# Rotated queries and keys added by TensorE, gates by Silu in one ScalarE pass

## The reference, cut to what matters

```
def _rope(x):
    ...
    x1, x2 = x32[..., : d // 2], x32[..., d // 2:]
    return jnp.concatenate([x1 * cos - x2 * sin, x1 * sin + x2 * cos], axis=-1).astype(x.dtype)

rq = _rope(proj[..., o_rq:o_rk].reshape(b, s, RET_HEADS, RET_HEAD_DIM))
rk = _rope(proj[..., o_rk:o_rv].reshape(b, s, RET_HEADS, RET_HEAD_DIM))
ret = _retention(rq, rk, rv)
ret = (_rms(ret) * ret_out_gain[l]).reshape(b, s, RET_WIDTH) * jax.nn.silu(r_gate.astype(jnp.float32))
...
return (o * jax.nn.silu(r)) @ w_out      # GLA, o is normalised and scaled by norm_g
```

## Time and profile before

| | |
|---|---|
| median of 3 runs | 991.39 us (990.47 to 992.85) |
| profiled execution, its own time | 991.15 us |
| its span, first to last instruction | 989.2 us |
| mean granted TensorE clock | 0.993 |
| busy: PE, DVE, ACT, POOL | 97%, 68%, 47%, 6% |

### The profile page before, as it was taken

How to read it: one execution, slowest core, us unless ns; L and a number is a source line. 1 busy time by engine, 2 the same in 40 slices (tenths; PEclk the granted TensorE clock), 3 DMA queues, 4 the chain that set the end, 5 groups by cost and what they waited for, 6 DMA issues and landing times.

```text
span 989.2 us, 13707 instructions
## 1 busy us (share of the span) xinstructions
PE 958.2 (97%) x4982; PEld 797.0 (81%) x4982; DVE 675.2 (68%) x875; ACT 463.4 (47%) x710; POOL 55.0 (6%) x61
## 2 busy tenths in 40 slices
PE   9999999999999999899899999998999999999996
PEld 7778877888888887777688888887776888888885
DVE  5868898895566576677976556667643876655657
ACT  5477535464445345544355444444652434544441
POOL 3040111200000001000200000000000010000000
PEclk9999999999999999999999999999999999999998
DMA  9979787596555676421375665564342537566541
GB/s 303 336 227 276 220 255 235 198 313 210 194 170 193 206 258 165 128 86 46 121 246 192 196 204 174 190 211 153 127 148 86 168 132 233 193 197 205 170 148 43
DMA packets 110053, 186.91 MB, mean 189 GB/s; under 512 B 8729, under 2 KB 67169, under 8 KB 109985
## 3 DMA queue, kind: packets, MB, share of 16 engines
q1 hardware_dynamic: 104800, 177.33, 55.1%
q0 software_dynamic: 2656, 8.54, 3.2%
q10 hardware_dynamic: 2544, 0.35, 0.2%
HBM read 185.15 MB, written 1.05 MB: 188 GB/s over the span
## 4 chain that ended last, share of the span: by engine, by line
PE 78%; DVE 11%; ACT 3%; issue 3%; DMA 2%; POOL 2%; SPq 0%; POOLq 0%; DVEq 0%; ACTq 0%
PE AT L1956 16%; PE PJ L1816 14%; PE PJ L1817 14%; PE PJ L1818 14%; PE AT L1960 8%; DVE wlo L1137 3%; POOL rstd L483 2%; ACT whi L600 1%; PE AT L1802 1%; DVE bn L1225 1%; DMA raw<-in_w_out_dram 1%; DMA raw<-in_w_ada_dram 1%; PE AT L1816 1%; PE AT L2065 1%; DVE x L1223 1%
## 5 line engine op out<-in xcount | busy, mean ns | idle before, releaser
L1137 DVE TENSOR_TENSOR wlo<-raw,whi 128x1024 fp32r<-128x1024 f32 x144 | 173.4, 1221 | 50.9 <-ACT whi L600 50.1
L1956 PE MATMUL AT<-hT,whi 128*128 128x512 f32 x720 | 179.5, 391 | 0.0
L1263 DVE TENSOR_TENSOR wlo<-raw,whi 128x1024 fp32r<-128x1024 f32 x144 | 169.6, 1219 | 0.0
L600 ACT ACTIVATE whi<-raw 128x1024 fp32r<-128x1024 f32 x144 | 146.6, 1054 | 40.1 <-DMA raw<-in_w_in_dram 28.8
L1816 PE MATMUL PJ<-whi,uhi 128*128 128x512 f32 x392 | 154.0, 393 | 0.4
L1817 PE MATMUL PJ<-wlo,uhi 128*128 128x512 f32 x392 | 153.0, 390 | 0.0
L1818 PE MATMUL PJ<-whi,ulo 128*128 128x512 f32 x392 | 152.6, 389 | 0.0
L1956 PEld LDWEIGHTS AT<-hT,whi 128*128 128x128 f32 x720 | 131.9, 188 | 25.3
L1816 PE MATMUL PJ<-whi,hT 128*128 128x512 f32 (+1 forms) x360 | 146.7, 407 | 4.7 <-DVE hT L1320 1.6
L1273 DVE TENSOR_TENSOR pr<-AT,pr 128x512 f32<-128x512 f32 x45 | 31.1, 691 | 169.0 <-ACT pr L655 169.0
L647 ACT ACTIVATE whi<-raw 128x1024 fp32r<-128x1024 f32 x144 | 140.7, 1049 | 0.3 <-DMA raw<-in_mlp_w_dram 0.3
(11 more groups left out here) (332 smaller groups left out, 995.9 us busy)
## 6 DMA issues: line engine op xcount, KB each, us to landing
raw<-in_mlp_w_dram SPq DMA_DIRECT2D x128, 512.0 KB, 4.8
raw<-in_w_in_dram SPq DMA_DIRECT2D x32, 512.0 KB, 6.4
raw<-in_w_ada_dram SPq DMA_DIRECT2D x32, 512.0 KB, 5.6
raw<-in_w_mlp_in_dram SPq DMA_DIRECT2D x32, 512.0 KB, 4.9
raw<-in_w_mlp_out_dram SPq DMA_DIRECT2D x32, 512.0 KB, 4.7
raw<-in_c_w_in_dram SPq DMA_DIRECT2D x24, 512.0 KB, 4.5
raw<-in_w_ada_dram SPq DMA_DIRECT2D x32, 256.0 KB, 6.6
raw<-in_a_w_in_dram SPq DMA_DIRECT2D x12, 512.0 KB, 5.2
```

The source lines that it names most:

```text
L600: nc.scalar.activation(whi[:, s % SPL, :], raw_slot(r), ACT.Copy).then_inc(hi_done, 1)
L1137: tt(wlo[:, n % SPL, :], raw_slot(r), whi[:, n % SPL, :].bitcast(F32), ALU.subtract).then_inc(raw_done, 1)
L1263: tt(wlo[:, s % SPL, :], raw_slot(r), whi[:, s % SPL, :].bitcast(F32), ALU.subtract)\
L1956: mm(out(f), whi[:, s % SPL, c(kk, f)], hT[:, k, :, :].rearrange("p a s -> p (a s)"), start=k == 0, stop=False, skip_group_check=True)
```

## The change

- `rotate` writes the cos part straight to `proj` and the sin part to `sc[:, t]`, and no longer adds them. For the keys it first waits for `rt_tr` (the turned queries of that tile), since `sc` is read by PE now; for the same reason ScalarE's `fox_squares(1)` waits for `rt_tr`.
- `turn` makes, per head, two fp32 matmuls with the identity that add up in PSUM, in place of one transpose.
- ScalarE computes Silu in place of Sigmoid for the retention and GLA gates and frees the PSUM banks itself. On DVE `ret_gates` goes, `r_gain` reads the finished gate from `proj`, and `gated` goes.

```diff
+            def silu(z, e):
+                return nc.scalar.activation(e, z, ACT.Silu)
             def gate_table():
-                gate(cst[:, C_ID:C_ID + 1], junk[:, :])
+                silu(cst[:, C_ID:C_ID + 1], junk[:, :])
...
                 act.wait_ge(sc_free, 4 + t)
+                if t:
+                    act.wait_ge(rt_tr, 1)
...
-                    gate(bank(7, t), proj[:, t, RG:RG + 512]).then_inc(gt_sig, 1)
+                    silu(bank(7, t), proj[:, t, RG:RG + 512]).then_inc(bank_free[1], 1)
...
-                    gate(bank(B_CIN + 4 + j, t), r_at(j, t)).then_inc(gt_sig, 1)
+                    silu(bank(B_CIN + 4 + j, t), r_at(j, t)).then_inc(bank_free[j], 1)
...
-                    a = sc[:, 0, :].rearrange("p (h d) -> p h d", h=4)
-                    c = sc[:, 1, :].rearrange("p (h d) -> p h d", h=4)
+                    a = proj[:, t, dst:dst + 512].rearrange("p (h d) -> p h d", h=4)
+                    c = sc[:, t, :].rearrange("p (h d) -> p h d", h=4)
+                    if k:
+                        dve.wait_ge(rt_tr, t + 1)
...
-                    link(tt(proj[:, t, dst:dst + 512], sc[:, 0, :], sc[:, 1, :], ALU.add))
...
-            def ret_gates():
-                for t in range(NT):
-                    o = proj[:, t, FK:FK + 512]
-                    dve.wait_ge(gt_sig, t + 1)
-                    tt(o, o, bank(7, t), ALU.mult).then_inc(bank_free[1], 1)
...
-                    dve.wait_ge(gt_sig, 2 + 2 * j + t + 1)
-                    tt(out_at(j, t).rearrange("p (h d) -> p h d", h=2),
-                             logit(j, t).rearrange("p (h d) -> p h d", h=2),
+                    dve.wait_ge(bank_free[j], B_CIN + 4 + t + 1)
+                    ins = tt(out_at(j, t).rearrange("p (h d) -> p h d", h=2),
+                             r_at(j, t).rearrange("p (h d) -> p h d", h=2),
...
-            def gated(j, t):
-                dve.wait_ge(gt_sig, 2 + 2 * j + t + 1)
-                tt(out_at(j, t), out_at(j, t), r_at(j, t), ALU.mult).then_inc(src_ready, 1)
...
-                    ins = nc.tensor.transpose(AT[:, f % 2, h * P:(h + 1) * P], proj[:, t, c0 + h * P:c0 + (h + 1) * P],
-                                              ident)
+                    o = AT[:, f % 2, h * P:(h + 1) * P]
+                    mm(o, proj[:, t, c0 + h * P:c0 + (h + 1) * P], ident, start=True, stop=False)
+                    ins = mm(o, sc[:, t, h * P:(h + 1) * P], ident, start=False, stop=True)
```

More of the change, by code:

```diff
@@ L260, in block_program @@
         dseq, aseq = sem("dseq"), sem("aseq")
-        gt_sig = sem("gt_sig")
         ffT_mm, ffT_done, ff_mm, ff_abs, ff_ln, ff_done, cum_mm, cum_done = [sem(n) for n in (
@@ L1474, in _ @@
                 28: [lambda: decayed(2), lambda: decayed(3)],
-                30: [ret_norm], 31: [ret_gates, ret_final],
+                30: [ret_norm], 31: [ret_final],
             })
@@ L1732, in _ @@
             r_at = lambda j, t: proj[:, t, 2048 + 512 * j:2048 + 512 * (j + 1)]
-            logit = lambda j, t: bank(B_CIN + 4 + j, t)
             out_at = lambda j, t: proj[:, t, half(j)]
@@ L1739, in r_gain @@
                 for t in range(NT):
-                    dve.wait_ge(gt_sig, 2 + 2 * j + t + 1)
-                    tt(out_at(j, t).rearrange("p (h d) -> p h d", h=2),
-                             logit(j, t).rearrange("p (h d) -> p h d", h=2),
-                             acc[:, NG:NG + 256].unsqueeze(1).broadcast_to([P, 2, 256]), ALU.mult).then_inc(bank_free[j], 1)
-                dve.wait_ge(bank_free[j], B_CIN + 4 + NT)
+                    dve.wait_ge(bank_free[j], B_CIN + 4 + t + 1)
+                    ins = tt(out_at(j, t).rearrange("p (h d) -> p h d", h=2),
+                             r_at(j, t).rearrange("p (h d) -> p h d", h=2),
+                             acc[:, NG:NG + 256].unsqueeze(1).broadcast_to([P, 2, 256]), ALU.mult)
+                link(ins)
             def gla_norm(j, t):
@@ L1753, in gla_norm, with gla_norms @@
                     ins = stt(o, AT[:, 2 * t + j, c], rstd[:, k:k + 1], o, ALU.mult, ALU.mult)
-                return ins
-            def gated(j, t):
-                dve.wait_ge(gt_sig, 2 + 2 * j + t + 1)
-                tt(out_at(j, t), out_at(j, t), r_at(j, t), ALU.mult).then_inc(src_ready, 1)
-            def gated_first():
-                for t in range(NT):
[L1763 to L1769, removed]
+                ins.then_inc(src_ready, 1)
+            def gla_norms(j):
+                for t in range(NT):
+                    gla_norm(j, t)
             tiles(T_CIN, T_COUT, {
@@ L1773, in _ @@
                 16: [lambda: state(0)], 17: [lambda: state(1)], 18: [lambda: state(2)],
-                19: [lambda: r_gain(0), lambda: gla_var(0)], 20: [lambda: gla_var(1), gated_first],
+                19: [lambda: r_gain(0), lambda: gla_var(0)], 20: [lambda: gla_var(1), lambda: gla_norms(0)],
                 22: [lambda: quarter_lo(7, 0), lambda: quarter_lo(7, 1)],
-                23: [lambda: r_gain(1), norm_second, lambda: gated(1, 0), lambda: gated(1, 1)],
+                23: [lambda: r_gain(1), lambda: gla_norms(1)],
             })
```

## The result

The changed kernel takes 995.07 us (median of 22 runs, 992.00 to 997.86); the kernel before, timed beside it, 992.57 us (22 runs, 989.95 to 994.93). The ratio is 1.0023, 95% interval [1.0013, 1.0033]. Over all three, the mean of its 46 runs is 994.84 and that of 116 runs of the kernel before is 992.85: +2.0 us, ratio 1.0020 [1.0015, 1.0026] (interval by resampling single runs, which leaves out the scatter between series). Taken by series, the means are 995.14, 994.52 and 994.61 with the change and 992.55, 992.34, 992.96, 994.02 and 993.38 without: each of the first lies above each of the second, and the difference of the two averages is +1.7. The change makes the kernel slower by 1.5 to 2 us; the forecast was +0.4 and a time of 991.8, and 995.07 is outside its range.

The account below looks back on a forecast made before the run. TensorE, busy 97% of the span, bounds the kernel. +5.3 - 2.5 - 1.7 = +1.2 us at 140 us, of which +0.4 reaches the end: 991.39 + 0.4 = 991.8 us, range 990.1 to 994.1.

Parts of the forecast that it names:

- the delay at the end of the first block: Rescaled x entering the first MLP: of PE's +1.2 us, DVE's own delay of +0.1 to +1.0 remains, taken at +0.4.
- the clock's credit: TensorE at 136 to 140 us: with no idle in front, the clock stays at 2.4 GHz, -1.7 us.
- PE's added work: Four turns of queries and keys: 32 product pairs at 0.217 us replace 16 transposes at 0.10, +5.3 us.
- The wait: PE's wait for DVE's rotation at the keys' turns goes entirely, -2.5 us, because PE is late, not only DVE early.
- rival 1: The clock falls all the same, at 136 to 140 us or nearby: 993.2 to 994.1 us, chance 0.13.
- PE's two waits: Ahead of the first MLP, for the rescaled x: 0.67 and 0.75 us start to start, absorbing part of PE's delay.
- rival 2: Before the first MLP, the last w_out tile lands later and PE waits instead: +1.0 to +2.5 us, chance 0.11.
- rival 3: By the first MLP all is hidden or a little gained, -0.2 at most by PE alone: 990 to 991.3, chance 0.13.
- rival 5: The change doesn't do what it says in the turns, adds and multiplies; given no chance.
- Gates: Silu removes 1.2 us of DVE multiplies at 163.61, offsetting DVE's +1.2 delay; the later GLA gates give nothing.
- The distance from M to the end: From the first MLP on the delay stays; wrong if it differs by over 0.5 us between 200 us and the end.

Follow-up runs that it names:

- e10: Changed kernel with only the keys turned by products, queries added and transposed as before, no filler products, GpSimd's two layer-norm broadcasts later: 992.86 us, ratio 1.0.
- e1: The kernel before once more, no edit: 994.35 us, ratio 1.0023 to the runs of the same kernel beside it.
- e6: The kernel before with GpSimd's two layer-norm row broadcasts issued later, behind its reciprocal roots: 991.85 us, ratio 0.999.
- e7: The kernel before with only the Silu gates of the change, and GpSimd's two layer-norm row broadcasts issued later: 992.28 us, ratio 0.9989.
- e12: The kernel before once more, no edit, a later repeat: 992.59 us, ratio 1.0005 to the kernel before.
- e4: The kernel before with only the Silu gates of the change, turns and rotation as before: 993.16 us, ratio 1.0013.
- e5: The changed kernel with GpSimd's two layer-norm row broadcasts issued later, behind its reciprocal roots: 992.79 us, ratio 1.0002.
- e3: The kernel before with only the turns by products and the rotation's sum of the change, gates as before: 993.83 us, ratio 1.0024.
- e2: The changed kernel once more, no edit: 994.82 us, ratio 1.0023 to the kernel before.
- e11: The changed kernel once more, no edit, a later repeat: 994.49 us, ratio 1.0014 to the kernel before.

## Why the prediction was wrong, point by point

In short: the term that failed is the delay at the end of the first block, taken at +0.4 us and measured at +1.35 in the two profiles that answer each other. Beside it the clock's credit of 1.7 us comes in some executions only, and 1.2 us of the miss in the total is the level of the three runs that the forecast started from.

**PE's added work, right.** 16 products take 3.55 and 3.57 us, 0.222 each, where 0.217 was used. Four turns cost 7.12 - 1.6 = +5.5 against +5.3. Of what the Trainium skill ("TensorE: Matmul & The Clock Gate", Terms) says, the transpose mode four times faster for fp32, the runs show 0.222 / 0.10 = 2.2 here, and rival 4 has fallen.

**The wait, right in size, wrong in its reason.** It left PE's list, and PE asked for nothing that was not ready. The prediction said that it goes "because PE is late, not only because DVE is early". Its own numbers say otherwise: the first turn ready at 132.80 and the second at 134.4, while PE without any delay is through the filler at 133.04 and through the first turn, eight products at 0.217, at 134.8. e10, read above, agrees: there the wait of 1.94 came back in place of a filler of 2.15. So by these numbers the credit of 2.5 us is DVE's, and it would stand with the queries' turns left alone.

**The clock, half right.** In the changed kernel it is 1.00 over 136 to 144, so the 1.7 us came back against the profile that was read; rival 1 did not happen. PE at K6 is 24.06 - 22.72 = +1.34, forecast +1.2. But the fall was taken as a property of the kernel before. With the original turns and rotation it came in before, e1, e6 and e7 and stayed away in e12 and e4. Against e12 PE is 24.05 - 21.09 = +2.96 late. On the mean of the three executions of the kernel before (22.13) it is +1.9. A credit that comes in some of the executions was booked in full. Whether a turn by products "would even work for the clock" no run decides; in e10 the clock fell during such a turn, behind the idle of 1.94.

**What the end of the block absorbs, wrong: this is the step that failed.** The prediction let the two releases before the removed multiplies cost "up to 1 us", took +0.4, on the reason that the transfer "has most likely used part of the idle DMA before 166", and let PE's two waits absorb the rest. The mechanism was seen (tiles released later, so that more bytes stand in front of the last one) and mis-sized. The DVE request did come as forecast (50.00 behind Q before, 50.13 after, so +0.1), and ScalarE's squares at +1.3 for the forecast +1.2. But the idle DMA lies in front of the restart (share 0.00 over 162.31 to 163.31, 0.65 in the microsecond behind it), not between the restart and the tile. The whole restart moved with PE, from 46.0 to 47.5, the landing by 57.43 to 58.78 = +1.35 and M by +1.38. That term is +1.35 in place of +0.4. Windows from the request of the tile to its landing, before and after, show the bytes:

```profile
167.31:174.74 7.43, 7.43 (x35) 5.53 (x34) 6.91 (x7) 2.04 (x3) 0.21 (x1) 1.00 0.96 274
```
```profile
170.73:179.38 8.65, 8.65 (x40) 6.58 (x39) 6.91 (x7) 2.98 (x4) 0.21 (x1) 1.00 0.98 314
```

That is 7.43 x 274 = 2.0 MB before and 8.65 x 314 = 2.7 MB after: 0.7 MB more had to pass, where up to 0.3 was counted. PE's two waits absorbed nothing, 0.53 and 0.59 as against 0.51 and 0.58, because what they wait for moved as much as PE did. This is rival 2 (+1.0 to +2.5, chance 0.11), as it was described. The agreement of +1.34 at K6, +1.35 at L and +1.38 at M is partly the luck of the pair: on the means of three executions each it is +1.9 at K6, +1.5 at L (57.34 to 58.82) and +1.5 at M, and against e1 alone L moves by just the +0.4 that was forecast. So of the mean +1.5, about 0.7 is the clock's credit booked in full, if that is handed on whole, and the other 0.8 stands where +0.4 was taken (an estimate).

**The other rivals.** Nothing was hidden or gained (rival 3): Q to M is longer than in every execution of the kernel before. Its "-0.2 at most" took both waits of PE, 1.42 us, as slack; e5 and e6 show that PE alone gives +0.4, since with the transfers away one wait of 0.4 stays. The change does what it says (rival 5): the turns and the missing rows stand in the trace.

**Gates, right within what can be told.** From Q to M e3 agrees with the changed kernel within 0.2 us and e7 with e6 within 0.02, though K6 is 0.25 earlier in e7: DVE's saved 1.2 us only let a tile be asked for earlier that lands no earlier. The GLA half changes no distance (763.15 in e4, 763.18 before).

**The distance from M to the end, wrong as a test.** It differed by 1.3 between the two profiles, more than the 0.5 allowed. That is the low clock at 416, which e12 has without the change.

**The level.** The three runs that gave 991.39 were low: 22 runs of the same kernel have 992.57. Of the 3.3 us between 991.8 and 995.07, 1.2 are this, and 2.1 the change's (2.5 in that series for 0.4). With the right term (+1.4) the forecast would have been 992.8; with the clock's credit at its mean, +1.5 to +2, still slower by less than the bound or just at it. The difference between the marks (+1.5) and the times (+1.7 to +2.0) stays open: it may be scatter between series, or the clock falling less often or more often in stretches that three profiles do not sample. In the timed runs the mean granted clock is no lower with the change (0.9920 in the 24 runs of e2 and e11, 0.9912 in 105 runs of the kernel before), so the added time is not a slower clock.

## What to carry to other kernels

Where an engine's lateness meets a stretch of saturated transfers, ask what restarts the transfers and how many bytes stand between the restart and the tile that is waited for, not only when that tile is asked for: a restart that hangs on the late engine handed on most of its delay here, and waits further down absorbed none of it. Before a wait is said to vanish because an engine is late, work out where that engine would stand on time: here the wait was DVE's to remove, and 5.5 us of products were paid beside it. Filler in front of a wait goes only when the wait is gone with PE on time; taken out in e10, it brought back the wait and the low clock. A gain that comes from the clock has to be weighed by how often the low stretch is there in repeated profiles, and marks laid into several traces can tell a microsecond that the times of a kernel with 4 to 7 us between its fastest and slowest run do not, if there are enough executions of both kernels.

## What the runs showed of the hardware that I had not expected

A wait of about the same length ahead of the keys' turns (1.66 us in six executions, 1.94 in e10) was followed by a fall of TensorE's clock from 2.4 to 1.2 GHz in some executions and by none in others. Of seven executions with a wait of 1.6 us or more at this place five fell (before, e1, e6, e7, e10) and two did not (e4, e12); of seven without a wait none did there. At 416 to 424 us, where the programs are the same, the clock fell in nine of fourteen executions, in kernels of every kind. The time from the restart of the transfers to the landing of the last 512 KB tile was steadier in nine executions (11.2 to 12.8 us) than the tile's own time from issue to landing (7.43 to 10.09 us): a tile asked for earlier in a full stretch took longer (10.09 us in e4 against 7.58 in e3, at 47.2 and 51.3 behind Q).
